# Input units 2 to 9 of the recurrent stage: from three narrow products to one wide and one narrow

## What is computed

```python
h = modulate(rms_norm_2(x, mix_norm), sh_m, sc_m)
u = h @ w_in                                   # 1024 x 2560
a_b, a_c, a_x, r_gate, r_x = jnp.split(u, cuts, axis=-1)      # 512 features each
y_a = a_b * causal_depthwise_conv(a_c * a_x, conv_a_w)
xr = causal_depthwise_conv(r_x, conv_b_w) + conv_b_b
y_b = jax.nn.gelu(r_gate) * rg_lru(xr, ...)    # r, i = sigmoid(xr @ w); a = exp(c r); h_t = a h_(t-1) + b
x = x + g_m * (concatenate([y_a, y_b]) @ w_out)
```

## Time and profile before

| | us |
|---|---|
| median of 3 runs | 870.85 |
| lowest, highest | 870.77, 870.97 |
| profiled execution, its own time | 870.38 |
| its span in the profile | 868.2 |
| busy PE, DVE, ACT, POOL | 863.3, 715.0, 491.0, 113.9 |

### The profile page before, as it was taken

The page is one execution under the profiler, slowest core; times in us unless marked ns, Lnnn a source line. Parts: engine busy times, 40 slices in busy tenths (PEclk is TensorE's granted clock), DMA queues, the critical chain, the costliest instruction groups (busy, mean ns, idle before and its releaser), DMA issues.

```text
span 868.2 us, 13238 instructions
## 1 busy us (share of the span) xinstructions
PE 863.3 (99%) x4795; PEld 738.6 (85%) x4795; DVE 715.0 (82%) x742; ACT 491.0 (57%) x668; POOL 113.9 (13%) x70
## 2 busy tenths in 40 slices
PE   9999999999999999999999999999999999999998
PEld 6998878888888799988888888878777988888887
DVE  6699989898989897998988999787897866755656
ACT  6545666555556567756455455655666555545542
POOL 6000100021120025017010411003000001100000
PEclk9999999999999999999999999999999999999999
DMA  8978669998898475647989798536435476666661
GB/s 272 336 273 320 220 223 371 336 366 334 325 340 311 135 241 183 206 128 241 383 305 337 270 348 288 191 123 217 146 99 160 126 220 190 183 198 184 190 195 72
DMA packets 117252, 208.07 MB, mean 240 GB/s; under 512 B 7259, under 2 KB 81355, under 8 KB 112086
## 3 DMA queue, kind: packets, MB, share of 16 engines
q1 hardware_dynamic: 116710, 205.31, 69.6%
q10 hardware_dynamic: 304, 2.10, 0.7%
q0 software_dynamic: 192, 0.05, 0.0%
HBM read 206.39 MB, written 1.05 MB: 239 GB/s over the span
## 4 chain that ended last, share of the span: by engine, by line
PE 98%; DVE 1%; ACT 0%; issue 0%; POOL 0%; POOLq 0%
PE tp L2062 12%; PE ub L2062 12%; PE acc L1918 8%; PE acc L1921 8%; PE acc L1923 7%; PE tp L2064 6%; PE ub L2064 6%; PE acc L1879 5%; PE acc L1883 5%; PE acc L1882 5%; PE acc L2048 3%; PE acc L2049 3%; PE acc L2050 3%; PE tp L2140 2%; PE acc L2140 1%; PE tp L2244 1%
## 5 line engine op out<-in xcount | busy, mean ns | idle before, releaser
L1226 DVE TENSOR_TENSOR w_lo<-w_raw,w_hi 128x1024 fp32r<-128x1024 f32 x267 | 336.5, 1278 | 74.3 <-ACT w_hi L777 73.8
L777 ACT ACTIVATE w_hi<-w_raw 128x1024 fp32r<-128x1024 f32 x267 | 279.8, 1057 | 193.4 <-PE ub L2064 38.7
L2062 PE MATMUL tp<-aT,w_hi 128*128 128x512 f32 x432 | 135.9, 396 | 0.0
L2062 PE MATMUL ub<-aT,w_hi 128*128 128x512 f32 x432 | 135.4, 395 | 0.0
L1918 PE MATMUL acc<-w_hi,hT_hi 128*128 128x512 f32 x266 | 103.8, 390 | 0.0
L1921 PE MATMUL acc<-w_lo,hT_hi 128*128 128x512 f32 x266 | 103.6, 390 | 0.0
L1923 PE MATMUL acc<-w_hi,hT_lo 128*128 128x512 f32 x262 | 101.9, 389 | 0.0
L674 POOL PARTITION_ALL_REDUCE mod<-mod x16 | 67.6, 4236 | 253.5 <-PE tp L2064 118.0
L2064 PEld LDWEIGHTS tp<-aT,w_lo 128*128 128x128 f32 x432 | 81.2, 188 | 19.2
L2064 PEld LDWEIGHTS ub<-aT,w_lo 128*128 128x128 f32 x432 | 81.1, 188 | 18.9
L2064 PE MATMUL tp<-aT,w_lo 128*128 128x256 f32 x432 | 84.9, 278 | 0.0
(11 more groups left out here) (346 smaller groups left out, 1429.6 us busy)
## 6 DMA issues: line engine op xcount, KB each, us to landing
ada_raw<-in_l_ada_w SPq DMA_DIRECT2D x24, 1024.0 KB, 6.5
w_raw<-in_l_ffn_w_gate SPq DMA_DIRECT2D x44, 512.0 KB, 4.6
w_raw<-in_l_ffn_w_up SPq DMA_DIRECT2D x44, 512.0 KB, 4.4
w_raw<-in_l_ffn_w_down SPq DMA_DIRECT2D x44, 512.0 KB, 3.8
w_raw<-in_w_up SPq DMA_DIRECT2D x32, 512.0 KB, 4.8
w_raw<-in_w_down SPq DMA_DIRECT2D x32, 512.0 KB, 5.3
scratch<-in_l_ada_w SPq DMA_DIRECT2D x14, 1024.0 KB, 7.3
w_raw<-in_attn_w_qkv SPq DMA_DIRECT2D x24, 512.0 KB, 6.9
```

Source lines behind the costliest of these rows:

```text
L777: act.activation(rounded_part(v), w_raw[:, v % SLOTS, :], ACT.Copy).then_inc(hi_done, 1)
L1226: dve.tensor_tensor(rest_part(v), w_raw[:, v % SLOTS, :], rounded_part(v).bitcast(F32), ALU.subtract).then_inc(lo_done, 1)
L2062: pe.matmul(banks[f], rounded_part(v)[:, c[f]], aT[:, :, b, :], start=b == 0, stop=False)
```

## The change

Units 2 to 9 are multiplied by `project_T_wide` in place of `project_T`. For each block of 128 inputs and each of two groups of 128 features, the rounded weight is multiplied at once by the rounded operand and the operand's rest, which lie side by side, into a bank of 512 columns. The weight's rest goes by 256 columns as before. So a unit has 16 products of 512 columns and 16 of 256, in place of 48 of 256, and fills two whole banks instead of two half banks.

The two halves of a bank must be added. The new step F n does that for each unit: ScalarE copies the operand-rest half of the two banks into `uT` (128 x 512), and VectorE adds the other half to it in place (128 x 512). E 2, 3 and 4 are gone. E 1's gelu now reads and writes `uT`. The banks are: units 2, 5, 7 in `acc` 2 and 3; 4 and 6 in `acc` 0 and 1; 3 and 8 in `ub`; 9 in `tp`. As the gates' products use `ub` too, G 0 now waits for the sum of unit 3 (`win_sum` 2).

```diff
-LRU_STEPS = steps("""B6 U0 H2 L2 U1 H3 E0 L3 M6 U2 H4 T0 L4 C0 B7 U3 H5 E1 L5 U4 H6 G0 L6 M7 U5 H7 G1 D0 E2
-    L7 U6 H8 L8 I0 D1 U7 H9 L9 Q0 E3 P0 U8 H10 Y0 L10 R0 J0 U9 H11 E4 L11 K0 U10 H12 Z0 L12 Z1
+LRU_STEPS = steps("""B6 U0 H2 L2 U1 H3 E0 L3 M6 U2 H4 T0 L4 C0 B7 U3 F2 H5 L5 U4 F3 H6 E1 G0 L6 M7 U5 F4 H7 F5 G1 D0
+    L7 U6 H8 L8 I0 F6 D1 U7 H9 L9 Q0 F7 P0 U8 H10 Y0 L10 R0 F8 J0 U9 H11 L11 K0 F9 U10 H12 Z0 L12 Z1
     U11 H13 L13 U12 H14 U13""")
+        def win_banks(n):
+            return {3: ub, 8: ub, 9: tp}[n][:, :, :] if n in (3, 8, 9) else acc[:, 0:2, :] if n in (4, 6) else acc[:, 2:4, :]
+        def win_blocks(n):
+            b = 4 * WIN_CHUNKS[n // 2] + 2 * (n % 2)
+            return uT[:, b:b + 2, :]
 # ScalarE
                 elif step == "E" and n == 1:
-                    act.wait_ge(w_used, parts_to(U_WIN + 4))
+                    act.wait_ge(win_sum, 2)
-                elif step == "E":
-                    act.wait_ge(w_used, parts_to(U_WIN + 2 * n + 2))
-                    act.activation(uT[:, b:b + 4, :]..., blocks_of(banks), ACT.Copy).then_inc(lru_u, 1)
+                elif step == "F":
+                    act.wait_ge(w_used, parts_to(U_WIN + n + 1))
+                    act.activation(win_blocks(n), win_banks(n)[:, :, TOK:CH], ACT.Copy).then_inc(win_rest, 1)
 # VectorE
+                elif step == "F":
+                    dve.wait_ge(win_rest, n - 1)
+                    dve.tensor_tensor(win_blocks(n), win_blocks(n), win_banks(n)[:, :, 0:TOK], ALU.add).then_inc(win_sum, 1)
                 elif step == "P":
-                    dve.wait_ge(lru_u, 2)
+                    dve.wait_ge(win_sum, 6)
                 elif step == "Z" and n == 0:
-                    dve.wait_ge(lru_u, 3)
+                    dve.wait_ge(win_sum, 8)
 # TensorE
-                    if c == 3:
-                        pe.wait_ge(lru_gelu, 1)
-                    if c == 4:
+                    if 5 <= n < 8:
+                        pe.wait_ge(win_sum, {5: 1, 6: 3, 7: 4}[n])
+                    if n == 8:
                         pe.wait_ge(lru_i, 1)
-                    project_T(U_WIN + n, n % 2, ub_banks if c == 4 else [acc[:, 2 * (c % 2) + p, :] for p in range(2)])
+                    project_T_wide(U_WIN + n, [win_banks(n)[:, f, :] for f in range(2)])
...
-                        pe.wait_ge(lru_u, 2)
+                        pe.wait_ge(win_sum, 6)
...
                 elif step == "G":
                     pe.wait_ge(lru_xr, 1)
+                    if n == 0:
+                        pe.wait_ge(win_sum, 2)
```

More of the change, by code:

```diff
@@ L395, in block_program @@
         hT_lo_done = sem("hT_lo_done")
+        win_rest = sem("win_rest")
+        win_sum = sem("win_sum")
         lru_p = sem("lru_p")
@@ L401, in block_program @@
         lru_gelu = sem("lru_gelu")
-        lru_u = sem("lru_u")
         lru_tap = sem("lru_tap")
@@ L1058, in _ @@
                 elif step == "E" and n == 1:
-                    act.wait_ge(w_used, parts_to(U_WIN + 4))
+                    act.wait_ge(win_sum, 2)
                     b = 4 * WIN_CHUNKS[n]
-                    act.activation(uT[:, b:b + 4, :].rearrange("p (b a) n -> p b a n", a=2), blocks_of(acc[:, 2:4, :]),
-                                   ACT.Gelu_apprx_tanh).then_inc(lru_gelu, 1)
+                    act.activation(uT[:, b:b + 4, :], uT[:, b:b + 4, :], ACT.Gelu_apprx_tanh).then_inc(lru_gelu, 1)
                     act.preload_act_table_set("sigmoid_and_others")
```

## The result

The changed kernel took 876.06 us (875.85 to 876.22, 4 runs) against 870.91 (870.77 to 871.12, 4 runs): ratio 1.0065, 95% interval 1.0053 to 1.0077, or 5.2 us slower (3.4 were forecast). The direction was right and the size was not. The profiled execution took 876.22, its span is 874.2.

The account below looks back on a forecast made before the run. The stage was taken as PE-bound, held by VectorE at its end. 2.15 (wait at G 0) less PE's gains 0.6, 0.2, 0.2, plus copy 0.5 and sums 0.6, 0.55, 0.6 gave +3.4, so 874.2 us; range 871.3 to 876.4.

Follow-up runs that it names:

- small_sums_7_8_9: The changed kernel with the sums of units 7 to 9 cut to 4 of 256 columns in each of the unit's two blocks: 874.62 us, ratio 1.0043.
- wait_at_g0_alone: The kernel before, with G 0 on PE also waiting for both parts of L 6 on VectorE: 874.71 us, ratio 1.0055; run again 875.19 us.

## What to carry over

Where a change gives a fully busy PE a wait of 2.25 us or more, as here, price the wait and then the half clock that may follow it (1.7 us on top), and look at the granted clock of the windows behind it before anything else. A sum that splits off a wide product belongs where its engine waits for something other than PE; one ahead of an instruction that PE waits for costs its whole duration, until another engine is as late as it makes VectorE (here ScalarE at L 11). And where several executions of a kernel differ by more than they do for the kernel before, sort them by their mean clock first: a single profile may show either kind.

## What the hardware showed beside this

By the mean clock, the granted clock fell behind an idle time of 2.25 to 2.77 us in 16 of 21 executions, and never behind 1.64 or 1.70 (14 executions); behind the 1.43 us of the changed kernel its windows show no fall. The half clock began 1.3 us after PE had started again in one execution of the changed kernel and 0.6 after it in the other, 1.0 after it in `small_sums_7_8_9` and 0.3 in `wait_at_g0_alone` run again, and 1.7 us were lost each time. The Trainium skill ("TensorE: Matmul & The Clock Gate", section HAM oscillation — how this bites in real kernels) describes such a fall behind each wait for a transfer between bursts of products, for waits of some 3 to 5 us. The runs here show it behind shorter ones, and not in every execution. What decides between executions was not found out, and no idle time between 1.70 and 2.25 us was tried.
